# Reordering four places of a two-block transformer kernel: the turned tokens, the convolved rounds, the pooled vector, the last projection

## The chip, the core and the metric

The kernel runs on one core of a Trainium2 chip. The metric is the device time of one execution in microseconds. Five engines work side by side, each through its own stream of instructions, and wait for one another by semaphores: PE (TensorE, matmuls), DVE (VectorE), ACT (ScalarE), POOL (GpSimd) and SP, which here issues DMAs.

## The reference, cut to what matters

A token matrix of 1024 x 1024 runs through a first block (windowed attention, a state space branch, a squared-ReLU feed-forward) and then through a hybrid block. The change lies between the end of the first block and the output.

```
# end of the first block
f = jnp.square(jax.nn.relu(h @ w_ff_in[l])) @ w_ff_out[l]
x = x + rmsnorm(f, norm_mlp_post[l])
# hybrid block
h = _rmsnorm(x, norm_g)
p = h @ w_in
(u, v, z_a, x_b, b_g, c_g, z_b, x_c, z_c, g_a, g_b, g_c) = jnp.split(p, _split_points(), axis=-1)
y_a = (_gmlp_branch(u, v, ln_g, ln_b, w_s, b_s) * jax.nn.silu(z_a)) @ w_pa
y_b = (_shortconv_branch(x_b, b_g, c_g, conv_w, conv_b) * jax.nn.silu(z_b)) @ w_pb
y_c = (_pool_branch(x_c, w_pool, pool_scale) * jax.nn.silu(z_c)) @ w_pc
merged = (jax.nn.sigmoid(g_a) * y_a + jax.nn.sigmoid(g_b) * y_b
          + jax.nn.sigmoid(g_c) * y_c)
return x + merged @ w_o
```

`_shortconv_branch` computes `bg * (conv(cg * xb) + conv_b)` with three taps along the tokens. `_pool_branch` multiplies a difference of running means by `w_pool` and scales it. All values are float32.

## The kernel before

Every float32 product is made of three matmuls: each operand is split into a high part, rounded by an ACT copy, and a low part, which DVE gets by subtracting the high part. A weight panel therefore passes a DMA (`raw`), ACT (`hi`) and DVE (`lo`) before PE may use it, and a DMA loads a panel when the one two before it has been used up by `lo`. PSUM is four double banks A0, A1, X0 and X1, each with halves a and b; the list `FILLS` says which tile goes where and in which order PE finishes them. PE's `begin` waits until the bank's last tile has been read ("evicted"). Each engine's stream is written out by hand; no scheduler moves anything. A matmul is 128 x 128 by 512 columns, and 24 of them (8 parts of the contraction k, 3 matmuls each) fill half a tile.

**The end of the feed-forward and the turned tokens.** For each of eight groups m of 128 tokens PE makes two halves `fo` (line 2258 and on, 24 matmuls a group). DVE adds them to `F` (`f_add`, line 1620), scales (`f_scale`, 1643, then an add on 1645) and, one group later, normalises (`x2_norm`, 1649). ACT takes mean squares of both halves (`f_square`) and of the new x (`x2_square`, which also stores x by DMA), both on line 871; POOL makes reciprocal roots of them (`rstd`, 2499 and 2500). PE turns the normalised tokens (`t2_turn`, 2050, eight transposes) into A0 or A1, alternating; ACT copies the high part (`t2_high`, 879) and DVE subtracts (`t2_low`, 1388), which frees the bank. ACT's order in group m is `f_square(m, 0)`, `f_square(m, 1)`, `x2_square(m - 1)`, `t2_high(m - 4)`; DVE's is `f_add`, `f_scale(m - 1)`, `f_add`, `x2_norm(m - 2)`, `t2_low(m - 4)`. After the last group PE does turn 5, the first half of the tile `au` 0 (tokens 0 to 511), turn 6, half of the contraction of `au` 1, turn 7, and the rest. `half_passes` (2004, 2007, 2010) makes half a tile in three passes instead of in triples: high by high, low weights by high tokens, high weights by low tokens.

**The rounds.** Twenty panels of w_in (`SEVEN`, numbered 0 to 19) are each done in seven products j = 0 to 6 of 12 matmuls (`seven`, 2425 to 2427), 19 us a round. Round p takes the banks X1a, X1b and A0a or, if p is odd, A1a, A1b and X0a: j = 0, 2, 4 and 6 share the first. ACT copies j = 0 to 2 out (1207), DVE adds a copy to j = 3 to 5 (1812) and multiplies where the branch asks for it (1816). Rounds 12 to 15 and 16 to 19 make the first and second half of branch b, with the kinds x, c, b and z (n = 0 to 3): n = 1 makes the product cg * xb, n = 2 begins with its convolution (`convolve`, 1776 and 1778, for two parts of 128 channels) and multiplies by bg, n = 3 the gate, and the next round multiplies it in (`b_gate`, 1825). The buffer `Y` has four parts: 0 and 1 hold x, later the convolution and the product, and 2 and 3 hold c times x, later the gate. `b_store` (712) stores parts 0 and 1 to `bv_scr`; the next round n = 0 waits for that store.

**The pooled vector.** PE makes `pl` 0 to 3 (2445 to 2447). For each j, DVE scales into `Gm` (1885), ACT copies the high part `BH` (1265), DVE subtracts to `BL` (1888). The merging tiles `cp` 0 to 7 follow, 24 matmuls each (contraction of four parts), and `cp` 0 waits for the low parts one by one.

**The last projection.** `w3` m = 0 to 7, one tile for 128 tokens, 48 matmuls in two halves n. The first waits for the low parts `NL` (1892) k by k. Tiles 0 and 1 are done half by half, (0, n = 0), (1, n = 0), (0, n = 1), (1, n = 1); the others whole.

## Time and profile before

| | us |
|---|---|
| median of 3 runs | 2210.7 |
| lowest, highest | 2208.86, 2211.46 |
| the profiled execution | 2210.0 |
| its span, first to last instruction | 2208.2 |
| PE busy | 2151.8 (97%) |
| DVE, ACT, POOL busy | 1048.8, 696.5, 265.4 |
| mean granted TensorE clock | 0.991 |

The span is what the trace shows, and 1.8 us lie around it. Times in the trace count from the span's start. A row of a timeline names start and duration in us, engine, line, operation, out<-in and count; in brackets stand the engine's idle time before it and who released it. The clock is a share of 2.4 GHz: 0.5 is 1.2 GHz.

### The profile page before, as it was taken

How to read it: one execution, taken by the hardware profiler on the slowest of the kernel's cores; microseconds unless marked ns; L12 is line 12 of the kernel's file. 1: busy time of each engine (PE TensorE's matmuls, PEld its weight loads, DVE VectorE, ACT ScalarE, POOL GpSimd, SP SyncE). 2: the span in 40 equal slices, each digit the busy share in tenths (PEclk: the TensorE clock that was granted, in tenths of full speed). 3: DMA queues.
4: the chain of work that ended last, by engine and by line, in shares of the span. 5: the costliest groups of instructions: out<-in, count | busy, mean ns of one | idle time of the engine just before them, and what ended most of it. 6: DMA issues, size and time to landing. Idle time of an engine off the chain costs nothing.

```text
span 2208.2 us, 24365 instructions
## 1 busy us (share of the span) xinstructions
PE 2151.8 (97%) x9972; PEld 1777.6 (81%) x9972; DVE 1048.8 (47%) x1170; ACT 696.5 (32%) x988; POOL 265.4 (12%) x507
## 2 busy tenths in 40 slices
PE   7999999989999999999999998999999989999998
PEld 6888888867888888888888877888888867878877
DVE  4226665847432233333233276665444546535452
ACT  4246666143323302102112043224444332222121
POOL 1376294000100000000000030200000000000100
PEclk9999999999999999999999999999999999999999
DMA  6542333675411102012012052113233211414332
GB/s 159 108 108 91 110 115 116 164 267 185 140 43 58 58 19 77 20 58 77 20 58 77 24 196 91 39 54 111 103 115 115 77 58 46 159 67 172 115 130 89
DMA packets 161922, 214.50 MB, mean 97 GB/s; under 512 B 26099, under 2 KB 127124, under 8 KB 161556
## 3 DMA queue, kind: packets, MB, share of 16 engines
q1 hardware_dynamic: 152336, 190.28, 26.5%
q10 hardware_dynamic: 9476, 22.67, 3.2%
q8 instruction: 79, 1.29, 0.2%
q14 instruction: 31, 0.25, 0.0%
HBM read 164.03 MB, written 47.71 MB: 96 GB/s over the span
## 4 chain that ended last, share of the span: by engine, by line
PE 84%; DVE 6%; issue 5%; ACT 2%; DMA 2%; SPq 1%; POOL 1%; DVEq 0%; POOLq 0%; ACTq 0%
PE A L1996 11%; PE A L1997 11%; PE A L1998 11%; PE X L2258 6%; PE X L2260 6%; PE X L2259 6%; PE A L2425 3%; PE A L2426 3%; PE A L2427 3%; PE X L2425 3%; PE X L2426 3%; PE X L2427 3%; PE A L2258 2%; PE A L2260 2%; PE A L2259 2%
## 5 line engine op out<-in xcount | busy, mean ns | idle before, releaser
L1341 DVE TENSOR_TENSOR WL<-raw,WH 128x1024 fp32r<-128x1024 f32 (+1 forms) x134 | 145.0, 1083 | 293.7 <-ACT WH L836 293.6
L1996 PE MATMUL A<-XBH,WH 128*128 128x512 f32 x616 | 240.1, 390 | 0.5 <-DVE WL L1341 0.5
L1998 PE MATMUL A<-XBH,WL 128*128 128x512 f32 x616 | 239.7, 389 | 0.0
L1997 PE MATMUL A<-XBL,WH 128*128 128x512 f32 x616 | 239.6, 389 | 0.0
L836 ACT ACTIVATE WH<-raw 128x1024 fp32r<-128x1024 f32 (+1 forms) x134 | 122.3, 913 | 281.2 <-PE A L1998 164.8
L2258 PE MATMUL X<-W2H,H 128*128 128x512 f32 x512 | 199.6, 390 | 0.0
L2260 PE MATMUL X<-W2H,H 128*128 128x512 f32 x512 | 199.2, 389 | 0.0
L2259 PE MATMUL X<-W2L,H 128*128 128x512 f32 x512 | 199.2, 389 | 0.0
L1112 ACT ACTIVATE HS<-A 128x1024 f32<-128x1024 f32 x32 | 32.8, 1024 | 401.0 <-PE A L1998 395.1
L1996 PE MATMUL A<-XH,WH 128*128 128x512 f32 x384 | 151.7, 395 | 0.0
L1620 DVE TENSOR_TENSOR F<-F,X 128x512 f32<-128x512 f32 x112 | 75.7, 686 | 156.3 <-PE X L2260 154.3
L1998 PE MATMUL A<-XH,WL 128*128 128x512 f32 x384 | 149.6, 390 | 0.0
L1997 PE MATMUL A<-XL,WH 128*128 128x512 f32 x384 | 149.5, 389 | 0.0
L1996 PEld LDWEIGHTS A<-XBH,WH 128*128 128x128 f32 x616 | 115.7, 188 | 25.0 <-issue 1.1
L1998 PEld LDWEIGHTS A<-XBH,WL 128*128 128x128 f32 x616 | 115.6, 188 | 24.1
L1997 PEld LDWEIGHTS A<-XBL,WH 128*128 128x128 f32 x616 | 115.7, 188 | 23.7
L1630 DVE TENSOR_TENSOR HS<-HS 128x1024 f32<-128x1024 f32 x32 | 39.2, 1224 | 171.7 <-ACT HS L1112 171.7
L2260 PEld LDWEIGHTS X<-W2H,H 128*128 128x128 f32 x512 | 96.1, 188 | 20.0
L2259 PEld LDWEIGHTS X<-W2L,H 128*128 128x128 f32 x512 | 96.1, 188 | 19.8
L2258 PEld LDWEIGHTS X<-W2H,H 128*128 128x128 f32 x512 | 96.1, 188 | 19.8
L1355 DVE TENSOR_TENSOR WL<-S,WH 128x512 fp32r<-128x512 f32 x80 | 55.1, 689 | 75.4 <-ACT WH L860 74.9
L2676 POOL TENSOR_TENSOR M<-M,GB 128x1024 f32<-128x1024 f32 x4 | 9.6, 2394 | 650.7 <-DVE GB L1910 650.7
(532 smaller groups left out, 4644.8 us busy)
## 6 DMA issues: line engine op xcount, KB each, us to landing
raw<-in_w_in SPq DMA_DIRECT2D x49, 1024.0 KB, 5.4
raw<-in_w_ff_in SPq DMA_DIRECT2D x16, 1024.0 KB, 5.3
rawk<-in_w_ff_out SPq DMA_DIRECT2D x16, 1024.0 KB, 5.0
g_scr<-stage SPq DMA_DIRECT2D x24, 512.0 KB, 3.6
g_scr<-gst ACTq DMA_DIRECT2D x32, 256.0 KB, 2.8
x_scr<-xr ACTq DMA_DIRECT2D x16, 512.0 KB, 2.6
xr<-x_scr SPq DMA_DIRECT2D x16, 512.0 KB, 4.2
xtok<-in_x SPq DMA_DIRECT2D x8, 512.0 KB, 7.5
```

The source lines that it names most:

```text
L836: A(unit_home(WH[:, r % 2, 0:kb, :], key), unit_of(raw[:, SLOT[p], 0:kb, :], key, i), ACT.Copy).then_inc(w_hi, 1)
L1341: TT(unit_home(WL[:, r, 0:kb, :], key), unit_of(raw[:, SLOT[p], 0:kb, :], key, i), unit_home(WH[:, r, 0:kb, :], key).bitcast(f32), ALU.sub ...
L1620: TT(F[:, m, sl], F[:, m, sl], psum(("fo", c, n, m)), ALU.add).then_inc(evicted[BUF["fo", c, n, m]], 1)
L1996: mm(dst, WH[:, r, k, :], xh, start=(k == 0), stop=False)
L1997: mm(dst, WH[:, r, k, :], xl, start=False, stop=False)
L1998: return mm(dst, WL[:, r, k, :], xh, start=False, stop=(k == kb - 1))
L2258: mm(dst, xh, wh(k), start=(k == 0), stop=False)
L2259: mm(dst, xh, wl(k), start=False, stop=False)
L2260: last = mm(dst, xl, wh(k), start=False, stop=(k == kb - 1))
L2425: mm(psum(key), high[:, i, :], xh, start=opens and i == 0, stop=False, skip_group_check=not opens)
L2426: mm(psum(key), high[:, i, :], xl, start=False, stop=False, skip_group_check=not opens)
L2427: last = mm(psum(key), low[:, i, :], xh, start=False, stop=i == KW - 1, skip_group_check=not opens)
```

## The change

It moves instructions and buffers and computes the same. (1) ACT's `t2_high(m - 4)` stands between the two squares of group m, and `x2_square(7)` ahead of high parts 4 to 7. On PE the first half of `au` 0 comes ahead of turn 5 and is made in three passes, which need high parts 0 to 3 to start and low parts 2 and 3 for the last pass only; turn 6 moves behind the first half of `au` 1's contraction, next to turn 7. Here turn 4 moves too: it stood behind group 7 and now follows the half tile. (2) In the second half of branch b the two pairs of `Y` change roles, so that its x goes to the parts that held the first half's gate; round 16 waits for the products (`b_product`) instead of for their store, and round 17 waits for the store. The convolution is spread: its first step stands in n = 1 behind j = 5, the second behind j = 6, four in n = 2 at j = 0 and 1. SP issues `b_store(0)` ahead of the panel of round 18. (3) DVE scales `pl` j + 1 ahead of the subtraction of j, with four parts of `Gm`, and PE does `cp` 0 and 1 together, k = 0 to 2 of both before k = 3. (4) The first four tiles of `w3` do k = 0 to 3 of n = 0 one after the other, then k = 4 to 7, then n = 1.

```
-                    sp.dma_start(bv_scr[row:row + P, :], Y[:, h, :]).then_inc(vec_out, 16)
+                    sp.dma_start(bv_scr[row:row + P, :], Y[:, 2 * i + h, :]).then_inc(vec_out, 16)
...
             for p in range(2, len(SEVEN)):
+                if p == 18:
+                    b_store(0)
                 seven_panel(p)
                 if p - 2 < 12:
                     gate_store(p - 2)
-                if p == 18:
-                    b_store(0)
...
             for m in range(MT):
                 f_square(m, 0)
+                if m >= 4:
+                    t2_high(m - 4)
                 f_square(m, 1)
                 if m:
                     x2_square(m - 1)
-                if m >= 4:
-                    t2_high(m - 4)
-            t2_high(4)
-            t2_high(5)
             x2_square(7)
-            for m in range(6, MT):
+            for m in range(4, MT):
                 t2_high(m)
...
                     if n == 0 and j == 3:
-                        dve.wait_ge(vec_out, 96 if i else 64)
+                        dve.wait_ge(b_product if i else vec_out, 2 if i else 64)
                     if n == 1 and j == 3 and i:
-                        dve.wait_ge(b_product, 2 * i)
+                        dve.wait_ge(vec_out, 96)
...
-                    dst = Y[:, h + (2 if n else 0), :]
+                    dst = Y[:, 2 * (1 - i if n else i) + h, :]
                 TT(dst[:, cols], psum(key), (c1, c5, c2)[j - 3][:], ALU.add).then_inc(evicted[BUF[key]], 1)
                 if kind == "b" and n in (1, 2):
                     freed(dve, key)
-                    out = Y[:, h + (2 if n == 1 else 0), cols]
-                    mixed[0] = mark(TT(out, Y[:, 2 + h, cols], Y[:, h, cols], ALU.mult))
+                    X, G = Y[:, 2 * i + h, cols], Y[:, 2 * (1 - i) + h, cols]
+                    mixed[0] = mark(TT(G if n == 1 else X, G, X, ALU.mult))
+                    if j == 5 and n == 1:
+                        after(mixed[0])
+                        last[0] = convolve(2 * i, 2)
...
-                    if kind == "b" and n == 2 and j < 3:
-                        for h in range(2):
-                            if j:
-                                after(last[h])
-                            else:
-                                after(mixed[0])
-                                freed(dve, ("P", p - 1, 6))
-                            last[h] = convolve(h, 2 * i + h, 2 - j)
+                    if kind == "b" and n == 1 and j == 6:
+                        after(last[0])
+                        last[0] = convolve(2 * i, 1)
+                    if kind == "b" and n == 2 and j == 0:
+                        freed(dve, ("P", p - 1, 6))
+                        last[1] = convolve(2 * i + 1, 2)
+                        after(last[0])
+                        convolve(2 * i, 0)
+                    if kind == "b" and n == 2 and j == 1:
+                        after(last[1])
+                        last[1] = convolve(2 * i + 1, 1)
+                        after(last[1])
+                        convolve(2 * i + 1, 0)
...
+            def pool_low(j):
+                dve.wait_ge(branch_hi, 4 + j + 1)
+                TT(BL[:, j, :], Gm[:, j, :], BH[:, j, :].bitcast(f32), ALU.subtract).then_inc(branch_lo, 1)
+            dve.wait_ge(branch_lo, 4)
+            for j in range(4):
+                filled(dve, ("pl", j))
+                freed(dve, ("cz", j))
+                STT(Gm[:, j, :], psum(("pl", j)), psc[:, j:j + 1], Y[:, j, :], ALU.mult, ALU.mult
+                    ).then_inc(evicted[BUF["pl", j]], 1)
+                if j:
+                    pool_low(j - 1)
+            pool_low(3)
...
+            def first_lows():
+                for m in (2, 3):
+                    freed(pe, ("t2", m))
+            begin(("au", 0))
+            pe.wait_ge(w_lo, UNIT["au", 0] + 1)
+            pe.wait_ge(xt_hi, 2 * MT + 4)
+            half_passes(("au", 0), xb, 0, lambda: None, first_lows)
             t2_turn(4)
             t2_turn(5)
-            for b in ("X0a", "X0b"):
-                free_of(b, ("au", 0))
-            first_half(("au", 0), xb, "t2", 0)
-            t2_turn(6)
             for b in ("X1a", "X1b"):
                 free_of(b, ("au", 1))
             first_half(("au", 1), xb, "t2", 0, range(KW))
+            t2_turn(6)
             t2_turn(7)
             first_half(("au", 1), xb, "t2", 0, range(KW, KD))
...
-                for f in range(8):
+                if s == "c":
+                    two_tiles(("cp", 0), ("cp", 1), branch, lambda k: pe.wait_ge(branch_lo, n + k + 1))
+                for f in range(2 if s == "c" else 0, 8):
...
+            for ks in (range(KW), range(KW, KD)):
+                for m in range(4):
+                    w3_half(m, 0, ks)
+            for m in range(4):
+                end(w3_half(m, 1), ("w3", m))
+            for m in range(4, MT):
```

What stands on ACT for one group of tokens, before and then in the changed kernel. Line 871 with `junk_c` is a half's square, with `F` the x2 square; line 1132 is the store, line 879 the high part.

```order
L871 ACTIVATE junk_c,vec<-F 128x512 x2
L1132 DMA x_scr<-xr_5_168 128x1024
L871 ACTIVATE F,vec<-xr_5_168 128x1024
L879 ACTIVATE XBH<-A 128x8x128
L871 ACTIVATE junk_c,vec<-F 128x512 x2
```

```order
L871 ACTIVATE junk_c,vec<-F 128x512
L879 ACTIVATE XBH<-A 128x8x128
L871 ACTIVATE junk_c,vec<-F 128x512
L1132 DMA x_scr<-xr_5_168 128x1024
L871 ACTIVATE F,vec<-xr_5_168 128x1024
```

The high part moved from behind the store and the x2 square to between the two half squares.

On PE, what follows the last matmul of the feed-forward, before and now (line 2050 became 2059, lines 2004, 2007 and 2010 became 2013, 2016 and 2019):

```order
L2260 MATMUL X<-W2H,H 128x512
L2050 MATMUL A<-ident,F 128x128 x16
L1996 MATMUL X<-XBH,WH 128x512
L1997 MATMUL X<-XBL,WH 128x512
L1998 MATMUL X<-XBH,WL 128x512
```

```order
L2269 MATMUL X<-W2H,H 128x512
L2013 MATMUL X<-XBH,WH 128x512 x8
L2016 MATMUL X<-XBH,WL 128x512 x8
L2019 MATMUL X<-XBL,WH 128x512 x8
L2059 MATMUL A<-ident,F 128x128 x16
```

Turns 4 and 5 moved behind the half tile, which became three passes of eight.

On DVE, from the last sum of round 13 (or 17) to the first of the next round. Line 1355 (now 1353) makes the low part of weights, 1369 (now 1367) the sums of weights, 1776 and 1778 (now 1775 and 1777) are the steps of the convolution, 1792 is j = 6. Before:

```order
L1816 TENSOR_TENSOR Y<-Y 128x512
L1355 TENSOR_TENSOR WL<-S_201,WH 128x512
L1792 TENSOR_TENSOR Y<-A,Y 128x512
L1355 TENSOR_TENSOR WL<-raw,WH 128x512
L1355 TENSOR_TENSOR WL<-S_202,WH 128x512
L1776 TENSOR_SCALAR Y<-Y,vec 128x1024 x2
L1355 TENSOR_TENSOR WL<-S_203,WH 128x512
L1778 SCALAR_TENSOR_TENSOR Y<-Y,vec 128x1023 x2
L1355 TENSOR_TENSOR WL<-raw,WH 128x512
L1369 TENSOR_TENSOR S_200<-raw 128x512
L1369 TENSOR_TENSOR S_201<-S_200,raw 128x512
L1778 SCALAR_TENSOR_TENSOR Y<-Y,vec 128x1022 x2
```

In the changed kernel:

```order
L1814 TENSOR_TENSOR Y<-Y 128x512
L1775 TENSOR_SCALAR Y<-Y,vec 128x1024
L1353 TENSOR_TENSOR WL<-S_201,WH 128x512
L1792 TENSOR_TENSOR Y<-A,Y 128x512
L1353 TENSOR_TENSOR WL<-raw,WH 128x512
L1777 SCALAR_TENSOR_TENSOR Y<-Y,vec 128x1023
L1353 TENSOR_TENSOR WL<-S_202,WH 128x512
L1775 TENSOR_SCALAR Y<-Y,vec 128x1024
L1777 SCALAR_TENSOR_TENSOR Y<-Y,vec 128x1022
L1353 TENSOR_TENSOR WL<-S_203,WH 128x512
L1777 SCALAR_TENSOR_TENSOR Y<-Y,vec 128x1023
L1777 SCALAR_TENSOR_TENSOR Y<-Y,vec 128x1022
```

All six steps now stand ahead of the sums of weights of j = 2, two of them in the round before.

## Rows read from the trace of the kernel before

**Rows 1.** The page, part 1: busy time, share of the span, instructions of each engine.

```profile
PE 2151.8 (97%) x9972; PEld 1777.6 (81%) x9972; DVE 1048.8 (47%) x1170; ACT 696.5 (32%) x988; POOL 265.4 (12%) x507
```

**Rows 2.** PE's waits by line and releaser: us in total, times, longest us.

```profile
PE X L2425 <- DVE Y L1812: 9.8, 3, 6.1
PE A L2050 <- DVE XBL L1388: 9.4, 4, 6.5
PE X L1996 <- DVE BL L1888: 3.5, 3, 1.9
```

**Rows 3.** Timeline of PE, turns 3 and 5 and the three-pass half.

```profile
1324.26 1.06 PE L2050 MATMUL A<-ident,F 128*128 128x128 f32 x8 [1.06 <-DVE XBL L1388]
1325.08 0.47 PE L2258 MATMUL X<-W2H,H 128*128 128x512 f32 x1
...
1339.48 1.94 PE L2050 MATMUL A<-ident,F 128*128 128x128 f32 x8 [6.54 <-DVE XBL L1388]
...
1357.52 1.98 PE L2007 MATMUL X<-XBH,WL 128*128 128x512 f32 x8
```

**Rows 4.** Timeline of DVE and ACT in group 6, and low part 3.

```profile
1324.03 0.68 DVE L1620 TENSOR_TENSOR F<-F,X 128x512 f32<-128x512 f32 x1
...
1327.68 1.28 DVE L1649 SCALAR_TENSOR_TENSOR F<-xr,vec,pre 128x1024 f32<-128x1024 f32 x1
1327.80 0.63 ACT L871 ACTIVATE junk_c<-F 128x512 f32<-128x512 f32 x1 [2.33 <-DVE F L1620]
...
1329.46 1.01 ACT L879 ACTIVATE XBH<-A 128x1024 fp32r<-128x1024 f32 x1
...
1330.50 1.22 DVE L1388 TENSOR_TENSOR XBL<-A,XBH 128x1024 fp32r<-128x1024 f32 x1 [1.55 <-ACT XBH L879]
...
1338.11 1.23 DVE L1388 TENSOR_TENSOR XBL<-A,XBH 128x1024 fp32r<-128x1024 f32 x1 [1.54 <-ACT XBH L879]
```

**Rows 5.** Timeline of POOL, two reciprocal roots of group 4.

```profile
1308.48 0.22 POOL L2499 TENSOR_SCALAR vec<-vec 128x1 f32<-128x1 f32 x1
...
1309.44 1.32 POOL L2499 TENSOR_SCALAR vec<-vec 128x1 f32<-128x1 f32 x1
```

**Rows 6.** Windows: stretch, length, busy PE, PEld, DVE, ACT, POOL, PEclk, DMA share, GB/s.

```profile
1309.43:1355.71 46.28, 36.87 (x177) 30.29 (x176) 33.20 (x31) 18.16 (x34) 11.61 (x24) 0.89 0.32 109
...
1813.81:1819.48 5.67, 5.67 (x14) 4.46 (x14) 1.74 (x3) 0.15 (x1) 0.00 (x0) 0.51 0.01 3
1856.64:1861.10 4.46, 4.46 (x13) 3.53 (x13) 3.17 (x5) 0.00 (x0) 0.00 (x0) 0.62 0.00 0
1972.65:1984.86 12.21, 8.73 (x25) 5.67 (x25) 7.09 (x6) 3.17 (x3) 0.00 (x0) 0.72 0.15 55
2112.06:2119.75 7.69, 6.71 (x25) 4.28 (x25) 7.66 (x7) 5.06 (x4) 0.00 (x0) 1.00 0.90 300
```

**Rows 7.** Timeline, the convolved rounds 14 and 16: DVE, PE and SP's queue.

```profile
1762.72 2.47 DVE L1778 SCALAR_TENSOR_TENSOR Y<-Y,vec 128x1022 f32<-128x1022 f32 x2
...
1768.59 0.68 DVE L1812 TENSOR_TENSOR Y<-X,c 128x512 f32<-128x512 f32 x1
...
1769.33 0.50 PE L2425 MATMUL X<-TH,WH 128*128 128x512 f32 x1 [1.85 <-DVE Y L1812]
...
1798.62 1.22 DVE L1825 TENSOR_TENSOR Y<-Y 128x1024 f32<-128x1024 f32 x1
...
1801.45 0.37 SPq L472 DMA_DIRECT2D raw<-in_w_in  x1
...
1810.54 0.69 DVE L1812 TENSOR_TENSOR Y<-X,c 128x512 f32<-128x512 f32 x1 [7.78 <-DMA bv_scr<-Y]
```

**Rows 8.** Timeline, the first part of the pooled vector: DVE and ACT.

```profile
1968.77 1.28 DVE L1885 SCALAR_TENSOR_TENSOR Gm<-X,vec,Y 128x1024 f32<-128x1024 f32 x1
...
1970.09 1.06 ACT L1265 ACTIVATE BH<-Gm 128x1024 fp32r<-128x1024 f32 x1 [1.07 <-DVE Gm L1885]
...
1971.25 1.23 DVE L1888 TENSOR_TENSOR BL<-Gm,BH 128x1024 fp32r<-128x1024 f32 x1 [1.20 <-ACT BH L1265]
```

More of the change, by code:

```diff
@@ L1215, in seven_act @@
                     elif n == 0:
-                        act.wait_ge(vec_out, 96 if i else 64)
-                        dst, func = Y[:, 1, :], ACT.Copy
+                        act.wait_ge(b_product if i else vec_out, 2 if i else 64)
+                        dst, func = Y[:, 2 * i + 1, :], ACT.Copy
                     else:
-                        dst, func = Y[:, 3, :], ACT.Silu
+                        dst, func = Y[:, 2 * (1 - i) + 1, :], ACT.Silu
                     A(dst[:, 0:HALF], psum(key), func).then_inc(evicted[BUF[key]], 1)
@@ L1264, in _ @@
                     freed(act, key)
-                    A(BH[:, j, :], Gm[:, j % 2, :], ACT.Copy).then_inc(branch_hi, 1)
+                    A(BH[:, j, :], Gm[:, j, :], ACT.Copy).then_inc(branch_hi, 1)
             def high_m(f):
@@ L1771, in _, with convolve @@
             PAIRS7 = len(SEVEN)
-            def convolve(n, j, tap):
-                G, out = Y[:, 2 + n, :], Y[:, n, :]
+            def convolve(j, tap):
+                i, h = j // 2, j % 2
+                G, out = Y[:, 2 * (1 - i) + h, :], Y[:, 2 * i + h, :]
                 if tap == 2:
@@ L2465, in w3_half @@
                 return token_tile(psum(("w3", m))[:, sl], last_tokens, lambda k: W3H[:, k, sl], lambda k: W3L[:, k, sl], m,
-                                  (lambda k: pe.wait_ge(m_lo, k + 1)) if m == 0 and n == 0 else None)
-            for n in range(2):
-                for m in range(2):
-                    last = w3_half(m, n)
-                    if n:
-                        end(last, ("w3", m))
-            for m in range(2, MT):
+                                  (lambda k: pe.wait_ge(m_lo, k + 1)) if m == 0 and n == 0 else None, ks=ks)
+            for ks in (range(KW), range(KW, KD)):
[4 more added lines that the diff above has]
+            for m in range(4, MT):
                 first = w3_half(m, 0)
```

34 lines of the change are left out of this document (13 added, 21 removed).

## The prediction

> **What bounds the kernel now.** I read the busy shares first: PE is busy for 97% of the span [rows 1], so what can be won is PE's waits and the matmuls that run slowly behind them. The second view is the list of PE's waits [rows 2]: DVE is the releaser of almost all, and the three largest entries from the end of the feed-forward on are edited places. The third is the timeline around each. Two quantities serve everywhere. A matmul that follows another starts 0.227 us after it: the eight of the pass that starts at 1355.71 are followed by the next pass at 1357.52 [rows 3, 6]. Its own row lasts 0.39 us, so a gap that a row calls 1.85 us costs 0.16 us more, 2.01 us. And behind a pause the granted clock can be 0.5, the 1.2 GHz level, where a matmul takes 0.2 us more: the window behind the longest pause of the rounds shows 0.51 [rows 6].
>
> **Part 1, the turned tokens (t2).** From turn 1 at 1309.43 to the three-pass half of `au` 0 at 1355.71, PE takes 46.28 us [rows 6]. In it are 72 matmuls of `fo`, 48 of `au` and seven turns (0.8 us each, from the start of one to the next row's start [rows 3]): 120 x 0.227 + 7 x 0.8 + 0.4 for slightly longer first matmuls = 33.2 us. So 13.1 us are lost: 6.54 + 0.16 at turn 5 [rows 3], 3.4 at the three other waits of the same entry (9.4 less 6.5 in all [rows 2], and 0.16 each), the rest in the slow stretch behind turn 5.
> Why PE waits: in DVE's round, `f_add`, `f_scale`, the add and the second `f_add` take 3.65 us, `x2_norm` 1.2, then DVE is idle for 1.55 us, released by ACT's high part, and the low part takes 1.15 [rows 4]. The round lasts 7.6 us, PE's own is 24 x 0.227 + 0.8 + 0.1 = 6.3. ACT does the high part last, behind both squares and the `x2` square, though the turn was done long before; ahead of the second square ACT is idle for 2.33 us [rows 4], and a high part is 1.0. Moved there, it costs ACT nothing, and DVE's round is 6.1 us, below PE's. I carry the rounds on with these durations, from m = 4: low part 3 goes from 1338.11 [rows 4] to 1331.6, and PE, which needs 6.3 us a round from turn 1 on, finishes `fo` at 1309.43 + 3 x 6.33 = 1328.4.
> Then PE takes the new half tile. Its first pass needs high parts 0 to 3: the last starts at 1328.1 and lands at 1329.2, a pause of 0.8. The two passes without the low part take 3.6 us, to 1332.8, just when low part 3 lands; the third ends at 1334.7. Turns 4 and 5 have nothing to wait for; `au` 1's first half of k runs to 1339.1, turn 6 has its low part 4 at 1338.9. Turn 7 needs low part 5, which on DVE stands behind low part 4 and `x2_norm(7)`: 1338.9 + 1.2 + 1.2 = 1341.3, a pause of 1.4 that the old order did not have, since it put 12 matmuls between turns 6 and 7. Behind it `au` 1's second half ends at 1344.9, against 1355.71. What is lost is then 2.2 us: gain **10.8**.
>
> A rule that speaks against a denser DVE: GpSimd makes the reciprocal roots on which `f_scale` and `x2_norm` wait. The first of its two instructions takes 0.22 us beside a DVE instruction that reads PSUM, but 1.32 when it starts beside `f_scale`, with two inputs in SBUF [rows 5]; the second behaves likewise. In the new order those for `f_scale` fall on the low part, one of whose inputs is in PSUM, and I let them cost nothing; the other answer is rival C. The Trainium skill (GPSIMD Engine Reference, 1. Specifications) says the same, that GpSimd shares its SBUF interfaces with VectorE and contends with two-input SBUF instructions; by it alone every one of the added collisions would count, and the sum would be rival C's.
>
> **Part 2, the convolved rounds.** Three stalls, all released by DVE's `seven_dve`: 9.8 us, of which the longest has 6.1 [rows 2], so 1.85 for each of the others.
> - Rounds 14 and 18: the six convolution steps (at most 1.24 us each, two in 2.47 [rows 7]) all stand in front of DVE's sum j = 4, which frees the bank of j = 6. It starts at 1768.59, and PE starts at 1769.33, 0.74 later [rows 7]; without a wait PE would have started 2.01 earlier, at 1767.32. Loss 2.01 + 0.12 (a first matmul of 0.50) and, in round 18, 2.01 + 1.74 (12 matmuls in 4.46 us [rows 6], less 2.72). Now the first step stands in round 13 behind j = 5, the second behind j = 6, four in j = 0 and 1 of round 14, none in j = 2. Those places have room: what sets DVE's time there is ACT's high parts, which go by PE. With the steps chained at 1.24 and the low parts between them at 0.6, DVE is done with the sixth step at 1760.9 instead of 1765.2. Eight instructions of 0.6 to 0.72 us follow (two weight subtractions, four sums of weights, the add and the product of j = 3): 5.2 us. I get the sum j = 4 to 1766.1, PE can go at 1766.8: 0.5 us before it asks. Nothing is left, with a thin margin.
> - Round 16: DVE waits 7.78 us for the DMA that stores the products, before it overwrites them [rows 7]. With swapped buffers it only waits for the products, the last of them from 1798.62 to 1799.84, before DVE comes there at 1810.54 - 7.78 = 1802.76 [rows 7]. Loss removed: 6.27, and 13 matmuls at 1.2 GHz in 5.67 us less 2.95 [rows 6] = 2.72. What is late next: the store is awaited in round 17 at about 1821, a full round after it was issued, and it took under 8 us: hidden. The store is now ahead of panel 18 on SP's queue; that panel was issued at 1801.45 for its slot's sake [rows 7], and the products are there before: 0.
> Gain 2.13 + 8.99 + 3.75 = **14.9**. The convolution itself keeps its instructions and durations.
>
> **Part 3, the pooled vector.** `cp` 0, 24 matmuls, takes 12.21 us instead of 5.44 [rows 6], since each of the four parts runs as a chain of scale on DVE, copy on ACT (+1.32), subtraction on DVE (+1.16), next scale (+1.14): 3.62 us a part [rows 8]. Now the next scale runs before the subtraction; DVE alternates at 2.35 us a part. Subtractions start at 1971.3, 1973.7, 1976.0 and 1977.3, and PE follows 1.27 later (the subtraction's 1.23 [rows 8] and the signal). PE, which now does k = 0 to 2 of two tiles before k = 3 of either, waits 0.9 in front of k = 1 and 0.9 in front of k = 2, and no more. `cp` 2's weights are released by the end of `cp` 0, which comes later in this order: 0.4 us of wait, the only new one. 6.8 - 2.4 = **4.4**.
>
> **Part 4, last projection.** `w3` 0 meets the low parts of k = 4 to 7 one by one: 7.69 us instead of 5.44 [rows 6]. Four half contractions (10.9 us) in front of k = 4 cover DVE's last low parts, done by 2118.9. The wait in front of the first matmul stays; it is for weights. The eighth tile and the tail behind it are as before. Gain **2.1**. Tile 0 ends 8.7 us later, which only moves evictions that had over 8 us to spare.
>
> Sum 10.8 + 14.9 + 4.4 + 2.1 = 32.2. Against the profiled execution's 2210.0 that is 2177.8; the median of the runs is 0.7 higher: **2178.5**. The places follow one another on PE with 40 us and more between them, so they add.
>
> **Rivals.**
> - A (forecast) as summed, 2176 to 2181: chance 0.55.
> - B, the clock falls in pauses that stay: 1.4 us at turn 7, twice 0.9 at `cp` 0. For it: pauses of 1.85 were followed by the full clock once and by 0.62 once [rows 6, 7]. Against it: turn 3's wait of 1.06 us was followed by turn and matmuls at full speed [rows 3]. A slow stretch cost 1.7 to 2.7 us; with one or two, 2180 to 2184. Chance 0.22.
> - C, DVE or GpSimd is later than I have it. If the small GpSimd instructions stretch, twice 1.1 less 0.5 of slack in each of three rounds, +5; if the margin of 0.5 in rounds 14 and 18 is missed, up to 2 each: 2180 to 2184. Chance 0.12.
> - D, the change does not do what it says in round 16, because the wait was not the store's: then 9.0 stay, 2187. The products' end at 1799.84 excludes nearly everything else: 0.02.
> - E, the pauses I left are covered too (a low part sooner than I add it up): 2175. Chance 0.07.
> - F, slower than before: with its breaks gone PE works without pause from 1309 on, and the chip grants 1.2 GHz under load. A matmul then costs 0.2 us more, and from 160 slow matmuls in all the gain is gone; 200 would give 2218. Speaking against it: the profiled execution stood at the full clock through stretches of more than 100 us without a wait, and fell only behind pauses. 0.01, and 0.01 for the rest.
>
> **Range and chances.** 2174.5 to 2184 takes in A, B and most of C and E and leaves out D, F and tails of C. Faster or slower by 0.2% is 4.4 us, about what a measurement of this kernel can tell from no change: every case but F is faster. 0.985, 0.005, 0.01.
>
> **What would show it.** Part 1: high parts between the squares, no DVE idle of 1.55 in the rounds, one pause of about 1.4 in front of the last turn. Part 2: no PE wait on the line of `seven_dve`, and no DVE wait for the store. Part 3: two pauses just under 1 us. Part 4: no waits on the low parts. Wrong would be a granted clock of 0.5 after 1309 anywhere (B), or a PE wait in rounds 14 and 18 (C).

## The result, and the profile after

| | before | changed |
|---|---|---|
| median | 2211.08 us (4 runs beside the changed kernel's) | 2178.48 us (4 runs) |
| lowest to highest | 2208.86 to 2216.84 | 2176.35 to 2181.27 |
| the profiled execution | 2210.0 | 2176.35 |
| its span | 2208.2 | 2174.6 |
| mean granted clock | 0.991 | 0.998 |

The ratio of the times is 0.9849, with a 95% interval of 0.9827 to 0.9872. The prediction was 2178.5. Beside other kernels the changed one was run again: 2179.69 (2179.21 to 2181.34), ratio 0.9852, 0.9837 to 0.9867.

First the busy shares of the changed kernel, in the form of [rows 1]:

```profile
PE 2140.1 (98%) x9972; PEld 1771.0 (81%) x9972; DVE 1047.2 (48%) x1170; ACT 696.0 (32%) x988; POOL 266.0 (12%) x507
```

The counts are those of [rows 1]: the same instructions, in another order. PE is busy for 11.7 us less although its work is the same, mostly because fewer of its matmuls ran at the lower clock.

The list of PE's waits (us in total, times, longest) on the lines of [rows 2]:

```profile
PE X L2005 <- DVE BL L1888: 1.3, 2, 0.7
PE A L2059 <- DVE XBL L1386: 1.2, 1, 1.2
PE X L2013 <- ACT XBH L879: 0.6, 1, 0.6
```

Of 22.7 us in [rows 2] 2.5 are left, with one wait on a high part that is new. The line of `seven_dve` is gone from the list.

PE's stream is the same up to the end of the feed-forward, so both traces can be cut at the same instructions. Lengths in us, from the start of one landmark to the start of the next:

| stretch | before | changed | gain | forecast | changed, run again |
|---|---|---|---|---|---|
| start to turn 1 | 1309.43 | 1306.65 | 2.8 | 0 | 1309.69 |
| turn 1 to the second half of `au` 0 | 46.28 | 35.78 | 10.5 | 10.8 | 35.80 |
| from there to the first `pl` | 611.50 | 597.46 | 14.0 | 14.9 | 597.11 |
| first `pl` to first `w3` | 144.85 | 140.69 | 4.2 | 4.4 | 140.83 |
| first `w3` to the last high matmul of `w3` | 88.63 | 86.46 | 2.2 | 2.1 | 86.46 |

(In the old order the second half of `au` 0 was the three-pass half of [rows 3]; in the new one it is the other half, with the same place in the work.) The four edited stretches give 30.9 where 32.2 was forecast. The 2.8 us in front of them belong to no edit: in the ten traces of this study turn 1 starts between 1306.15 and 1313.16, with the same instructions before it. The rounds scatter too: the five traces with the old rounds take 609.65 to 614.77 us from the second half of `au` 0 to the first `pl`, so the 14.0 of that row belongs to this pair of executions, and another pair can show 12 to 18. The other old stretches scatter less: 45.73 to 46.46, 144.85 to 145.03 (once 146.76) and 88.61 to 88.64.

**The turned tokens.** Timeline of PE in the changed kernel (start, duration, engine, line, operation, out<-in, count, in brackets idle time before and releaser):

```profile
1306.65 1.04 PE L2059 MATMUL A<-ident,F 128*128 128x128 f32 x8
...
1319.32 1.04 PE L2059 MATMUL A<-ident,F 128*128 128x128 f32 x8
1326.44 2.08 PE L2013 MATMUL X<-XBH,WH 128*128 128x512 f32 x8 [0.60 <-ACT XBH L879]
...
1332.07 1.91 PE L2059 MATMUL A<-ident,F 128*128 128x128 f32 x16
...
1336.56 1.03 PE L2059 MATMUL A<-ident,F 128*128 128x128 f32 x8
1338.76 1.06 PE L2059 MATMUL A<-ident,F 128*128 128x128 f32 x8 [1.17 <-DVE XBL L1386]
```

Turns 1 to 3 come every 6.33 us without a wait, where [rows 2] count four waits at turns. And DVE, ACT and POOL in the same rounds:

```profile
1311.08 0.22 POOL L2517 TENSOR_SCALAR vec<-vec 128x1 f32<-128x1 f32 x1
...
1313.34 1.01 ACT L879 ACTIVATE XBH<-A 128x1024 fp32r<-128x1024 f32 x1
...
1315.65 1.28 DVE L1647 SCALAR_TENSOR_TENSOR F<-xr,vec,pre 128x1024 f32<-128x1024 f32 x1
1315.76 0.63 ACT L871 ACTIVATE junk_c<-F 128x512 f32<-128x512 f32 x1 [1.42 <-DVE F L1618]
1316.84 1.22 DVE L1386 TENSOR_TENSOR XBL<-A,XBH 128x1024 fp32r<-128x1024 f32 x1
...
1329.97 1.32 POOL L2517 TENSOR_SCALAR vec<-vec 128x1 f32<-128x1 f32 x1
1331.37 1.52 POOL L2518 TENSOR_TENSOR vec<-vec 128x1 f32<-128x1 f32 x1
1332.92 1.28 DVE L1647 SCALAR_TENSOR_TENSOR F<-xr,vec,pre 128x1024 f32<-128x1024 f32 x1 [0.46 <-POOL vec L2518]
...
1335.06 1.22 DVE L1386 TENSOR_TENSOR XBL<-A,XBH 128x1024 fp32r<-128x1024 f32 x1 [0.86 <-ACT XBH L879]
...
1337.40 1.22 DVE L1386 TENSOR_TENSOR XBL<-A,XBH 128x1024 fp32r<-128x1024 f32 x1
```

The high part stands between the squares, and the low part follows `x2_norm` at once: the 1.55 us of idle time of [rows 4] are gone. The square still waits for `f_add`: 1.42 us, of the 2.33 of [rows 4].

**The rounds.** DVE and PE in round 14: the last two steps of the convolution, both of the second part, the sum j = 4, and PE at j = 6:

```profile
1745.14 2.60 DVE L1777 SCALAR_TENSOR_TENSOR Y<-Y,vec 128x1023 f32<-128x1023 f32 x2
...
1752.84 0.68 DVE L1810 TENSOR_TENSOR Y<-X,c 128x512 f32<-128x512 f32 x1
...
1753.83 0.39 PE L2443 MATMUL A<-XBH,WL 128*128 128x512 f32 x1
1754.05 0.39 PE L2441 MATMUL X<-TH,WH 128*128 128x512 f32 x1
```

The sum j = 4 starts at 1752.84. In [rows 7] PE followed such a start by 0.74, so the bank was to be had at 1753.58, and PE took it at 1754.05, in its own step of 0.22 behind the matmul before: a margin of 0.47, forecast 0.5.

Then round 16, the products, their store and the first sum:

```profile
1783.21 1.22 DVE L1827 TENSOR_TENSOR Y<-Y 128x1024 f32<-128x1024 f32 x1
...
1787.26 0.68 DVE L1810 TENSOR_TENSOR Y<-X,c 128x512 f32<-128x512 f32 x1
```

The sum stands there without a bracket, where [rows 7] had `[7.78 <-DMA bv_scr<-Y]`.

**One wait that nobody forecast**, in front of `cx` 0 just behind the last round: SP's queue, ACT, DVE and PE.

```profile
1843.58 1.13 SPq L472 DMA_DIRECT2D raw<-in_w_in  x2
...
1850.29 1.06 ACT L836 ACTIVATE WH<-raw 128x1024 fp32r<-128x1024 f32 x1 [7.88 <-DMA raw<-in_w_in]
1851.38 1.23 DVE L1339 TENSOR_TENSOR WL<-raw,WH 128x1024 fp32r<-128x1024 f32 x1 [3.96 <-ACT WH L836]
1852.75 0.47 PE L2005 MATMUL X<-XBH,WH 128*128 128x512 f32 x1 [0.62 <-DVE WL L1339]
```

And the same panel in the kernel before, where PE does not wait behind it:

```profile
1871.79 1.13 SPq L472 DMA_DIRECT2D raw<-in_w_in  x2
...
1877.25 1.06 ACT L836 ACTIVATE WH<-raw 128x1024 fp32r<-128x1024 f32 x1 [6.64 <-DMA raw<-in_w_in]
```

From issue to ACT's start it is 6.7 us in one trace and 5.5 in the other. The ten traces settle what decides: the panel lands 5.17 to 7.15 us after its issue, PE waits in the four in which that is over 6.1 (6.28, 6.36, 6.68 and 7.15 us, with waits of 0.23, 0.28, 0.62 and 1.09), and in each of them landing less wait is 6.05 to 6.08. That is the length of the cover.

**The pooled vector and the last projection.** Timeline of DVE and PE, then the first matmul of `w3`:

```profile
1944.02 1.22 DVE L1888 TENSOR_TENSOR BL<-Gm,BH 128x1024 fp32r<-128x1024 f32 x1
...
1946.34 1.21 DVE L1888 TENSOR_TENSOR BL<-Gm,BH 128x1024 fp32r<-128x1024 f32 x1
...
1947.61 0.50 PE L2005 MATMUL X<-BH,WH 128*128 128x512 f32 x1 [0.62 <-DVE BL L1888]
...
1949.94 0.50 PE L2005 MATMUL X<-BH,WH 128*128 128x512 f32 x1 [0.67 <-DVE BL L1888]
...
1958.63 0.47 PE L2005 MATMUL X<-BH,WH 128*128 128x512 f32 x1 [0.24 <-DVE WL L1339]
...
2080.58 0.47 PE L2267 MATMUL X<-W3H,NH 128*128 128x512 f32 x1 [1.07 <-issue]
```

DVE alternates at 2.33 us a part (1944.02 to 1946.34), where [rows 8] had a chain of 3.62. Two pauses are left at `cp` 0 and a short one at `cp` 2, as forecast. In `w3` no wait on a low part is left.

### The profile page after: what moved, and what is told of

Read it like the earlier page. It is cut to its first block, busy times and chain, and to the rows that moved or that the text cites. A ratio compares the mean times of both kernels' runs of the same rounds, so it can differ in the third digit from the quotient of the medians.

```text
span 2174.6 us, 24357 instructions
## 1 busy us (share of the span) xinstructions
PE 2140.1 (98%) x9972; PEld 1771.0 (81%) x9972; DVE 1047.2 (48%) x1170; ACT 696.0 (32%) x988; POOL 266.0 (12%) x507
## 4 chain that ended last, share of the span: by engine, by line
PE 86%; DVE 5%; issue 4%; ACT 2%; DMA 1%; SPq 1%; POOL 1%; DVEq 0%; POOLq 0%; ACTq 0%
PE A L2005 11%; PE A L2006 11%; PE A L2007 11%; PE X L2267 6%; PE X L2269 6%; PE X L2268 6%; PE X L2441 3%; PE X L2443 3%; PE X L2442 3%; PE A L2443 3%; PE A L2442 3%; PE A L2441 3%; PE A L2267 2%; PE A L2269 2%; PE A L2268 2%
```

## Experiments

Two theories stood against each other. Theory 1 is the prediction's: DVE's chains release PE, so each edit is worth the wait that it removes, and the buffer swap, the spreading of the convolution, ACT's order and DVE's order carry the gain. The rivals give the gain, or part of it, to the edits of PE's order alone, or to the clock, that is, to slow stretches which came and went by chance. "Changed kernel" is the kernel of the change; lengths are those of the table above.

### ACT's order alone

```
             for m in range(MT):
                 f_square(m, 0)
+                if m >= 4:
+                    t2_high(m - 4)
                 f_square(m, 1)
...
-                if m >= 4:
-                    t2_high(m - 4)
-            t2_high(4)
-            t2_high(5)
             x2_square(7)
-            for m in range(6, MT):
+            for m in range(4, MT):
                 t2_high(m)
```

> The kernel before with ACT's part of the turned tokens alone (high parts between the squares), PE's order as before. Theory 1 (DVE's round of 7.6 us with its 1.55 us of idle was the bound): the rounds fall to PE's 6.3 us, turn 5 waits 3.7 instead of 6.5 us, turns 6 and 7 do not wait; from turn 1 at to the three-pass half 37 us (40 if the clock falls behind turn 5), against 46.3 before and 35.8 with both. So 6.5 to 9.3 of the 10.5 us come from ACT's order. Rival 2 (the half tile ahead of turn 5 is what covers the wait): the stretch stays above 43 us.

Measured: 2204.89 (2202.09 to 2205.80), ratio 0.9963 (0.9951 to 0.9976). The one wait of PE at a turn that is left, timeline:

```profile
1333.52 1.07 PE L2048 MATMUL A<-ident,F 128*128 128x128 f32 x8 [3.45 <-DVE XBL L1386]
```

The three waits in the rounds are gone, and the 6.54 at turn 5 became 3.45. The stretch takes 37.14 us: 9.1 of the 10.5 come from ACT's order alone, in an execution in which the clock did not fall behind the 3.45; the expectation put up to 3 us on such a fall. The median fell by only 7.2. The profiled execution gave 3.3 us back in the rounds, which this edit doesn't touch (614.77 us to the first `pl`, where the kernel before had 611.50): both pauses of 1.85 us were followed by the lower clock, where before only one was, and PE waited 1.09 us in front of `cx` 0. Both vary without an edit, as the waits in front of `cx` 0 given above and the last part of this section show; how it went in the other five executions no trace shows.

### PE's order of the turned tokens alone

```
+            half_passes(("au", 0), xb, 0, lambda: None, first_lows)
             t2_turn(4)
             t2_turn(5)
...
-            first_half(("au", 0), xb, "t2", 0)
-            t2_turn(6)
...
             first_half(("au", 1), xb, "t2", 0, range(KW))
+            t2_turn(6)
             t2_turn(7)
```

> The kernel before with PE's part of the turned tokens alone: three-pass half tile ahead of turns 4 and 5, turn 6 next to turn 7; ACT's order as before, with high parts 4 and 5 ahead of the x2 square of group 7. Theory 1: the half tile needs high part 3, which lands at 1338.1 on the time scale of before; PE waits 7.4 us there instead of 6.5 at turn 5, runs slowly behind it, and turn 7 waits another 2 us for the x2 square that ACT does late; the stretch from turn 1 to the three-pass half takes 47 to 49 us, 1 to 3 us more than before: the PE order alone is a loss. Rival 2: the half tile covers the wait by itself, the stretch takes less than 43 us.

Measured: 2214.93 (2209.47 to 2218.90), ratio 1.0008 (0.9998 to 1.0019). Where PE stood, with ACT ahead of it:

```profile
1337.75 1.04 ACT L871 ACTIVATE F<-xr 128x1024 f32<-128x1024 f32 x1
...
1338.79 1.00 ACT L879 ACTIVATE XBH<-A 128x1024 fp32r<-128x1024 f32 x1
...
1339.94 2.47 PE L2004 MATMUL X<-XBH,WH 128*128 128x512 f32 x5 [7.40 <-ACT XBH L879]
```

The three-pass half tile in front now waits 7.40 us for high part 3, which ACT still makes last. The stretch takes 47.12, 0.8 more than before. PE's new order is worth nothing until ACT's order makes high part 3 early; then it adds the last 1.4 (37.14 to 35.78), and it leaves no pause as long as 3.45 behind which the clock could fall. The two parts of the edit do not add up: 9.1 and -0.8 alone, 10.5 together.

### The buffer swap without the spread convolution

```
-            dve.wait_ge(vec_out, 96 if i else 64)
+            dve.wait_ge(b_product if i else vec_out, 2 if i else 64)
...
-                    dst = Y[:, h + (2 if n else 0), :]
+                    dst = Y[:, 2 * (1 - i if n else i) + h, :]
```

with the same exchange of the pairs at the other places of branch b, and the store ahead of panel 18; the six steps stay in n = 2, two each at j = 0, 1 and 2.

> The kernel before with the exchanged buffers of the second half of branch b and the earlier store alone; the six convolution steps stand in the round of bg as before. Theory 1: the wait of 6.1 us in round 16 and the slow stretch behind it are gone, no DVE wait for the store anywhere; the two waits of 1.85 us in rounds 14 and 18 stay, with 0.1 to 1.8 us of slowness each. From the three-pass half to the first pl product 601.5 to 604 us, against 611.5 before and 597.3 with both. Rival 2 (the wait was for something else that comes back, say for the products in round 16 or the store in round 17): a wait of over 1 us in one of these rounds besides the two.

Measured: 2202.00 (2197.48 to 2204.81), ratio 0.9950 (0.9932 to 0.9967). PE's waits on `seven_dve`, the list's row:

```profile
PE X L2426 <- DVE Y L1812: 3.7, 2, 1.9
```

Of the three waits of [rows 2] (9.8 us, longest 6.1) the one in round 16 is gone, and the two of 1.85 stay. The stretch to the first `pl` takes 600.88 us, 10.6 less than before. Forecast for round 16 was 8.99; the other 1.6 are the slow stretch in round 18 (1.74, from 1856.64 in [rows 6]), which this execution did not have; so it came out a little under the 601.5 to 604 that were expected. So the wait was the store's, and rival D falls.

But this run holds two edits, and one rival to the swap was left untested: SP's order by itself. SP's queue in the kernel before, and then here:

```profile
1801.86 1.05 SPq L712 DMA_DIRECT2D bv_scr<-Y  x2
```

```profile
1800.64 3.06 SPq L712 DMA_DIRECT2D bv_scr<-Y  x2
1804.95 0.38 SPq L472 DMA_DIRECT2D raw<-in_w_in  x1
```

Before, the two stores are issued right behind the panel of 1801.45 in [rows 7] and land 7.31 and 7.92 us after their issue, the last at 1810.41, just ahead of DVE's sum. Here each goes out when its product is made, ahead of the panel, and lands 2.65 and 2.66 us after its issue. An estimate from these rows for the kernel before with the store ahead of panel 18 and nothing else: the second store goes out at 1799.87, behind the product that ends at 1799.84, and lands at 1802.5, where DVE comes to the sum at 1802.76. Then the wait of 7.78 us is gone without any exchange of buffers. No run shows it. So it is shown that the two edits together remove the wait, not that the swap is needed.

### The convolution's last steps back at j = 2

```
                     if kind == "b" and n == 2 and j == 0:
                         freed(dve, ("P", p - 1, 6))
                         last[1] = convolve(2 * i + 1, 2)
-                        after(last[0])
-                        convolve(2 * i, 0)
                     if kind == "b" and n == 2 and j == 1:
                         after(last[1])
                         last[1] = convolve(2 * i + 1, 1)
+                    if kind == "b" and n == 2 and j == 2:
+                        after(last[0])
+                        convolve(2 * i, 0)
                         after(last[1])
                         convolve(2 * i + 1, 0)
```

> The changed kernel with the last convolution step of both parts in j = 2 of the round of bg, one step fewer in j = 0 and in j = 1. The same six instructions ahead of the same sums. Theory 1 (what counts is the idle time of DVE in front of ACT-paced weights, which steps in j = 0 and 1 use and steps in j = 2 do not): DVE reaches the sum j = 4 of rounds 14 and 18 about 2.1 us later, past the margin of 0.47 us that the after trace shows; PE waits 1.5 us by the rows' count in each of the two rounds, and the stretch from the three-pass half to the first pl product is 3.3 us longer, up to 6 with a slow stretch, than 597.3. Rival 2 (it is the two steps in round 13 that remove the stall, and where the others stand does not matter): no wait, 597.3.

Measured: 2183.57 (2182.66 to 2185.71), ratio 0.9870 (0.9855 to 0.9884).

```profile
PE X L2442 <- DVE Y L1810: 3.1, 2, 1.6
...
1755.48 2.47 DVE L1777 SCALAR_TENSOR_TENSOR Y<-Y,vec 128x1022 f32<-128x1022 f32 x2
...
1761.35 0.68 DVE L1810 TENSOR_TENSOR Y<-X,c 128x512 f32<-128x512 f32 x1
...
1762.09 0.50 PE L2442 MATMUL X<-TH,WH 128*128 128x512 f32 x1 [1.57 <-DVE Y L1810]
```

Two steps, 2.47 us, put back in front of the sums of weights take up the margin of 0.47 and leave 2.0; PE shows a gap of 1.57, which with the 0.16 of its row is 1.73, in both rounds. The stretch takes 600.28 us, 2.8 and 3.2 more than in the two executions of the changed kernel; without their waits in front of `cx` 0 (0.62 and 0.28, 0.16 more each) the difference is 3.6, and twice 1.73 is 3.5. The margin in the changed kernel is therefore as thin as read: of the 2.47 us PE pays 1.73 in each round, the margin takes 0.47, and 0.27 are in no row. That two steps stand in round 13 isn't enough; where the others stand matters.

### DVE's order of the pooled vector alone

```
-                    TT(BL[:, j, :], Gm[:, j % 2, :], BH[:, j, :].bitcast(f32), ALU.subtract).then_inc(branch_lo, 1)
+            for j in range(4):
...
+                STT(Gm[:, j, :], psum(("pl", j)), psc[:, j:j + 1], Y[:, j, :], ALU.mult, ALU.mult
+                    ).then_inc(evicted[BUF["pl", j]], 1)
+                if j:
+                    pool_low(j - 1)
+            pool_low(3)
```

> The kernel before with the pooled vector's DVE and ACT part alone (scale of j + 1 ahead of the subtraction of j, four buffers), PE doing cp 0 whole as before. Theory 1 (the chain of 3.62 us a part was the bound, and PE's pairing of cp 0 and 1 adds nothing): two pauses of about 0.65 in the rows' count in front of k = 1 and 2, none in front of k = 3, no wait for the weights of cp 2; from the first pl product to the first w3 matmul 140.0 to 140.6 us, as much as or 0.4 less than with the pairing (140.7), against 144.85 before. Rival 2 (the pairing is needed): k = 3 waits too and the stretch is above 141.5.

Measured: 2206.19 (2202.11 to 2209.52), ratio 0.9974 (0.9964 to 0.9983). PE at `cp` 0:

```profile
1976.26 0.50 PE L1998 MATMUL X<-BH,WH 128*128 128x512 f32 x1 [0.61 <-DVE BL L1881]
1978.59 0.50 PE L1998 MATMUL X<-BH,WH 128*128 128x512 f32 x1 [0.67 <-DVE BL L1881]
```

The same two pauses as in the changed kernel, without the pairing of `cp` 0 and 1, and none at `cp` 2. The stretch takes 140.12 us, 0.6 less than the changed kernel's 140.69.

### The pairing of `cp` 0 and 1 alone

```
-                for f in range(8):
+                if s == "c":
+                    two_tiles(("cp", 0), ("cp", 1), branch, lambda k: pe.wait_ge(branch_lo, n + k + 1))
+                for f in range(2 if s == "c" else 0, 8):
```

> The kernel before with the pairing of cp 0 and cp 1 alone, DVE's and ACT's order of the pooled vector as before. Theory 1: the low parts come every 3.6 us; PE waits 1.9 and about 2 us in front of k = 1 and 2 and then has three parts of cp 1 to do while the last comes; from the first pl product to the first w3 matmul 142.5 to 144 us, against 144.95 before: the pairing helps only where the chain is slow, and with DVE's new order it is worth nothing. Rival 2: it is worth nothing here either.

Measured: 2211.29 (2206.09 to 2232.39, 10 runs), ratio 1.0005 (0.9983 to 1.0027): its runs scatter so far that the time tells nothing, and the stretch has to. It takes 143.31 us, 1.5 less than before. With DVE's old chain two waits (1.90 and 1.96) stay, where ACT's order alone, also at the full clock, left three (1.89, 1.96, 1.96), and `cp` 2 waits 0.24. So pairing is worth 1.5 us against the old chain, and once DVE alternates it costs 0.6, by one trace without it and two with it: the cover that it gives is no longer needed at k = 3, and the wait for `cp` 2's weights remains (0.24 and 0.16; the other 0.2 are spread over the stretch). Two edits with one aim don't add.

### The changed kernel again, and a version that covers the pauses that are left

> The changed kernel once more, to see what varies between executions. Theory 1 (the gain is the sum of waits removed from the turned tokens on): 30.9 us between the traces of before and after lie from turn 1 on (10.5 + 14.0 + 4.2 + 2.2), the other 2.8 us lie ahead of turn 1, where nothing was edited, and are chance; here turn 1 starts anywhere between 1306 and 1310, while the length from turn 1 to the three-pass half stays at 35.8 and from the first pl product to the first w3 matmul at 140.7, within 0.3. Rival 2 (the early part also became faster through the change): turn 1 starts at 1306.6 again. The wait of 0.6 in front of cx 0, which the after trace shows and I had not forecast: if it is the load of its panel by chance, it is 0 to 1 here and not the same; if the change causes it, it is 0.6 again.

This is the changed kernel as it is; the result stands above. The last kernel takes turn 4 ahead of the half tile, puts turn 7 in the middle of `au` 1's second part, and moves work between the pooled parts:

```
+            t2_turn(4)
             begin(("au", 0))
...
-            t2_turn(4)
             t2_turn(5)
...
             t2_turn(6)
+            first_half(("au", 1), xb, "t2", 0, range(KW, KW + 2))
             t2_turn(7)
-            first_half(("au", 1), xb, "t2", 0, range(KW, KD))
+            first_half(("au", 1), xb, "t2", 0, range(KW + 2, KD))
...
+POOLED = [("cx", t) for t in range(4)] + [("cz", 0), ("cz", 1), ("cz", 2), ("pl", 0), ("pl", 1), ("cz", 3), ("pl", 2), ("pl", 3)]
```

with `cp` 0 whole, and the load of `pl`'s weights behind the panels of `cx` on SP's queue.

> The changed kernel with what its own trace still shows taken away, each by an order: turn 4 ahead of the half tile (fills the wait of 0.6 for high part 3), turn 7 between k = 5 and k = 6 of au 1 (covers the 1.17 in front of it), pl 0 and 1 ahead of cz 3 (the low parts of the pooled vector have a whole tile of time), cp 0 whole instead of paired with cp 1, and the load of the pool weights behind the panels of cx. Theory 1 (every pause of PE is a wait for a chain that an order can hide): turn 1 to the three-pass half 33.7 us instead of 35.8, no pauses at cp 0 and no wait for cp 2's weights, from the three-pass half to the first w3 matmul 735.5 instead of 738.0; in all 4.5 us less than the changed kernel, about 2174 to 2175. Rival 2 (a pause only moves: turn 7's high part then holds up the high parts 6 and 7 of the second half tile, and pl 2 and 3 hold up cp 0): pauses of 0.5 to 1 appear there, and the gain is under 2 us.

Measured: 2174.18 (2172.82 to 2176.10), ratio 0.9826 (0.9812 to 0.9841), against 0.9849 and 0.9852 for the changed kernel: the best of all. The profiled executions differ by 1.4 us up to the second half of `au` 0 (34.42 and 35.78), and by 3.0 and 2.8 from there to the first `w3` (735.15 against 738.15 and 737.94). PE in the turned tokens:

```profile
1328.42 1.04 PE L2063 MATMUL A<-ident,F 128*128 128x128 f32 x8
1329.21 2.09 PE L2017 MATMUL X<-XBH,WH 128*128 128x512 f32 x8
...
1339.19 1.06 PE L2063 MATMUL A<-ident,F 128*128 128x128 f32 x8 [0.59 <-DVE XBL L1387]
```

Turn 4 fills the 0.6 us in front of the half tile, and the pause in front of turn 7 is gone; but with turn 4 out of the way turn 6 is reached 0.8 us sooner, and 0.59 of wait appears there. At `cp` 0 and 2 nothing waits. Part of the 3.0 us is the wait in front of `cx` 0, which is absent here; its panel landed 5.17 us after its issue, sooner than in any of the nine traces in which the load of `pl`'s weights goes just ahead of it (5.44 to 7.15). Whether the later load did that or chance is open, since the wait is absent in five of those nine too. The kernel holds five edits, and no run has them one by one.

### The same pause, two clocks

With the kernels that keep the convolution in place, six traces hold the same two pauses of 1.85 us (1.84 in one) in rounds 14 and 18. The granted clock in the 4 us behind them:

| | round 14 | round 18 |
|---|---|---|
| before | 1.00 | 0.57 |
| ACT's order alone | 0.61 | 0.57 |
| PE's order alone | 0.66 | 1.00 |
| DVE's order of the pooled vector alone | 1.00 | 1.00 |
| the buffer swap alone | 1.00 | 1.00 |
| the pairing alone | 1.00 | 0.57 |

Two windows of the kernel before, in the columns of [rows 6], show the pair:

```profile
1769.33:1773.33 4.00, 4.00 (x18) 3.31 (x19) 3.97 (x7) 0.63 (x1) 0.00 (x0) 1.00 0.00 0
1856.64:1860.64 4.00, 4.00 (x11) 3.17 (x12) 3.17 (x5) 0.00 (x0) 0.00 (x0) 0.57 0.00 0
```

18 matmuls started in 4 us at the full clock, 11 at the lower. Five of twelve pauses were followed by the fall. Of the longer ones, each of the five at turn 5 or the half tile (6.54, once 7.40) and of the five in round 16 (6.1 to 6.33) was followed by it. The wait of 3.45 in the kernel with ACT's order alone was not, nor that of 2.13 at turn 7 with PE's order alone, nor was any of the pauses of 0.6 to 1.6 us in the turned tokens and the rounds of the changed kernel, its second run, the closer version and the one with the late convolution. Ahead of turn 1 the same was there to be seen: a pause of 1.92 to 1.96 us near 485 us, which all ten traces have, was followed by the lower clock in six (0.57 to 0.62 in the 4 us behind it) and by the full clock in four.

## Why the prediction was right, step by step

**The gain as a whole.** The forecast gain was 32.2. The medians differ by 32.6, and by 32.35 in the second comparison (2212.04 and 2179.69). The profiled executions differ by 33.65 (2210.0 and 2176.35), of which 30.9 lie in the edited stretches and 2.8 ahead of them. So the time was met with 1.3 us less of gain in the edited stretches than summed, and the fit of the single execution owes something to chance ahead of turn 1. Rival A, the sum, holds.

**Part 1: forecast 10.8, measured 10.5.** The landing times were right to 0.2 us. Shifted by the 2.8 us of the earlier start, the forecast had low part 4 done at 1336.1 and low part 5 at 1338.5; the rows give 1336.28 and 1338.62. The pauses were 0.60 and 1.17 in the rows, 2.1 with 0.16 each, against 2.2. The 0.3 were lost elsewhere: 35.78 less 2.1 is 33.7 of work, where the step on the work had 33.2. Three rounds take 6.33 us each, 0.08 more than 24 x 0.227 + 0.8; the three passes 5.63 (1326.44 to 1332.07) instead of 5.45; and each half of `au` 1's tile some 2.84 instead of 2.72: 0.67 together, and with some 0.15 on the turns behind them 0.8, where 0.4 was allowed. That the largest share hangs on ACT's order was shown by the kernels with one order each; the prediction had told the mechanism but not split it.

**GpSimd.** In the rounds the small instructions stay short (0.22 at 1311.08, beside the low part), as the prediction had it from the place where they fall. At the last group they did stretch, 1.32 and 1.52 us, beside `f_scale` and the add, which both read SBUF twice, and DVE then waited 0.46 for them. By the Trainium skill (GPSIMD Engine Reference, 1. Specifications) the contention is with VectorE's instructions that take both inputs from SBUF, and these rows agree. By that rule a small instruction beside the low part, one of whose inputs is in PSUM, is no collision, and the rows bear it out; so the prediction was wrong to say that by the Trainium skill alone every added collision would count and the sum be rival C's. It cost PE nothing: the low part 4 behind it was held by ACT's high part (0.86), which stands behind `x2_square(7)`, and came when forecast.

**Part 2: forecast 14.9, measured 14.0.** The three stalls went as forecast; the margin of 0.5 was 0.47; the store in round 17 was waited for by nobody. The 8.99 of round 16 were credited to the swapped buffers, with the store's new place on SP's queue at 0; by the landings read above the new place alone may give them (an estimate), and no run tells the two apart. What was missing is one wait that the sum did not have: 0.62 + 0.16 in front of `cx` 0, by a panel that lands 6.7 us after its issue where it took 5.5 before. The cover there, some 6.06 us, is about as long as the landing, so it shows in some executions and not in others: 0, 0.62, 0.28, 1.09, 0, 0, 0, 0, 0 and 0.23 in the ten traces, two of the four waits in kernels whose edits don't touch this place. The step that was incomplete is "what is late next": it was asked of each removed stall, and not of the stretch behind the rounds, where a cover with no slack was left as it was. The rest, 0.1, is in no row.

One term was a lottery ticket: the 1.74 us of the slow stretch in round 18 and the 0 in round 14 were read off one execution. Five of twelve such pauses had it, so two pauses cost 1.4 to 1.5 us on average, close to the 1.74 by luck.

**Part 3: forecast 4.4, measured 4.2.** The two pauses (0.62 and 0.67 in the rows, 0.78 and 0.83 whole; forecast 0.9 each) and the 0.24 + 0.16 at `cp` 2 are there. The sum took off 2.4, though its own terms (twice 0.9, and 0.4) give 2.2; from the start of `cp` 0 to that of `cp` 2 the changed kernel takes 13.25 us, 2.35 more than 48 matmuls at 0.227, so the 2.4 fits, but 0.34 of it stands in none of the three waits, and the sum named nothing for it. What the prediction had wrong is the credit: it counted PE's pairing among what keeps the pauses small. DVE's order alone leaves the same two pauses and gives 4.7 us; the pairing takes 0.6 of it back (one trace each, so the 0.6 is the least certain figure here).

**Part 4: forecast 2.1, measured 2.2.** No wait on a low part is left, and the wait of 1.07 in front of the first matmul stayed, as told.

**The rivals.** B: the clock did not fall behind any of the pauses that were left, from turn 1 to the last matmul; over 1309 to 1960 us the mean of the changed kernel is 1.00:

```profile
1309.00:1960.00 651.00, 647.08 (x2969) 534.44 (x2968) 370.71 (x472) 228.64 (x353) 24.58 (x40) 1.00 0.27 94
```

The runs show falls behind pauses of 1.85 us and above, and none behind 1.6 or less at these places, so 0.22 was more than B deserved for pauses of 0.8 to 1.4. C: half of it came true, GpSimd stretched, at a place where it cost nothing; the margin held. D fell with the run of the buffer swap. E, pauses covered too, did not come by itself, but the closer version shows that it can be had: 2174.18, where E had 2175. F: 651 us of nearly unbroken matmuls at the full clock say that load alone does not bring the fall here.

## What to carry to other kernels

Where an engine's last instruction of a round releases the bottleneck, look for idle time of that engine earlier in the round and move it there; here the bottleneck's own reordering was worth nothing alone (-0.8 us at the turned tokens) or less than the other engine's (1.5 against 4.7 at the pooled vector). Of two edits that cover the same wait, measure each by itself in the finished kernel: the second may only cost. When a wait is for a DMA, look first at what its queue issues just ahead of it. A pause's price is its length and, from 1.85 us on in these traces, a chance of a slow stretch behind it, so compare edits by stretches between landmarks and not by one median, and after the big stalls are gone look at the covers that have no slack left.

## What the runs showed of the hardware

- The same pause of 1.85 us in the same place was followed by the full clock in seven cases and by the lower level, 1.2 GHz, for some 3 to 4 us in five. What decides was not found. How much of the scatter between executions of one kernel it explains is not shown: the buffer swap alone ran at 2197.48 and 2199.31 with a mean clock of 0.995, and at 2204.69 and 2204.81 with 0.991, but the trace of the last has the full clock behind both of these pauses, and its slow stretches elsewhere; and the changed kernel took 2176.35 and 2181.27 at the same mean clock of 0.998.
- A wait of 3.45 us at turn 5 was followed by the full clock, though shorter ones in the rounds were not. Length alone does not decide.
- Slow stretches inside a chain that DVE releases cost little or nothing: `pl` to `w3` takes 144.85 us in the kernel before, with a clock of 0.72 over `cp` 0 [rows 6], and 145.01 with ACT's order alone, at the full clock, whose waits are 1.89, 1.96 and 1.96. Only the swap's trace, with the lower clock at all three pauses, came out longer, 146.76.
- Two stores of 512 KB that SP issued right behind a panel of 1 MB landed 7.3 and 7.9 us after their issue (the kernel before, round 16); issued one by one ahead of the panel, each landed in 2.7 (the buffer swap alone).
- With the same instructions ahead of it, turn 1 starts anywhere from 1306.15 to 1313.16, and the traces show most of the reason. PE's wait in front of the first matmul of `X<-ZH,WH`, near 460 us, is absent in the earliest trace, 0.54 us in the changed kernel's, 1.86 to 2.05 in the three that reach turn 1 at 1309.4 to 1309.7, and 3.0 to 4.4 in the five latest; two of these, at 1312.95 and 1313.16, also wait 2.7 and 2.2 instead of 1.1 to 1.4 near 545 us. The profile names no releaser for the first of these waits, so what makes it long or short is open.
